# Leaving out the products of zeros on TensorE in a two-block network kernel on one core

## The chip, the core and the metric

The kernel runs on one NeuronCore of a Trainium2 chip. A core has a matrix engine (TensorE, called PE in the profile; its weight loads are the rows PEld), a vector engine (DVE), an activation engine (ACT), GpSimd (POOL) and SyncE (SP), which here only starts DMA transfers. Each engine has its own queue of instructions and runs it in order; the engines meet only at semaphores. The metric is the device time of one launch in microseconds. The shorter the better.

## The reference

The program is a chain of two small networks on 256 tokens of width 1024, all in fp32. Cut to what matters:

```
x = first_block(x)     # layer 0: gated mixer, PEER experts; layer 1: differential attention, PEER experts
x = second_block(x)    # retention + RWKV-7 mixer, cross attention to a memory, squared-ReLU MLP

h = rmsnorm(x, g) * (1 + scale) + shift          # ahead of every large product
p = h @ w_in                                     # large products: 1024 x 1536 up to 1024 x 4096
x = x + gate * (mixer(p) @ w_out)
x = x + gate * peer(h)                           # scores of 16384 experts by u, weighted sum of v
y = rmsnorm(x, norm_final)
```

Between the large products stand small ones (attention heads of 64 to 256 channels, a chunked linear recurrence with 64-step chunks, group norms), each of them bound to vector and activation work before and after it. Nothing in the reference asks for a product with zeros.

## The kernel before, in words

Activations stay in SBUF with channels on partitions and the 256 tokens along the free axis. A large product is a stream of weight tiles of 128 x 1024 (`linear`, lines 403 to 563; `peer_scores` and `peer_output` have the same stream written out). SP loads a tile into one of four slots, ACT copies it rounded to fp32r (line 265), DVE makes the rest (line 271), and PE multiplies high by high, high by low and low by high (line 399, 24 matmuls of 128x256 a tile; line 1367 for the experts' output).

The program is a list of blocks. At the end of a block all engines meet, and none starts on the next one before the last has come. In a row of the profile `<-PEq L1515` after a start means that PE's own queue was the last to reach the end of the block that was opened on line 1515. So the order of the work is that of the source, engine by engine, and a block is as long as its slowest engine.

The helper `keep_warm(count, bank)` (lines 227 to 231) issues `count` matmuls of a 128x128 matrix of zeros by 512 columns of a constant, into a PSUM bank that nobody reads. Nobody waits for them, and they wait for nobody, but they stand in PE's queue in order. Each appears in the trace as two records of line 231. There are 98 of them, in 34 places, of these kinds:

- At the end of `split` (line 390), three beside the rounding of a product's input, five times.
- In `linear` (line 469) one after the two matmuls L331 and L333 that add up squares over the channels, six times; likewise in `peer_output` (1388) and `norm_in_place` (1739). ACT turns the sum into a root (L342, L344), and the next large product then starts with its norm: DVE scales (L537), ACT rounds (L500), DVE makes the low part (L530 or L532), and PE follows channel block by channel block (L399).
- In `norm_in_place` (1737) one ahead of the sixteen records of L362 (eight matmuls with ones, which add up the squares); in `peer_output` (1380) one ahead of the transposes L786.
- In `block_rms` (line 1526, three or five at its end, behind L1524) and in the block that follows (L1577 in `odd_mixer`, L1842 in `retention`, L2213 in `rwkv`).
- In `rope` (1475) two at its end, behind the products L1473.
- In `rwkv` two ahead of the low-rank products L1898 to L1902 (1894), seven and twelve in the two blocks after them (1951, 1977), and in each of the two token tiles one ahead of L2114 and one ahead of L2123 (lines 2109 and 2117).
- In `setup` twelve, in `even_mixer` two and six.

In a token tile (`tile`, line 2026) the last block goes: L2103 and L2108, then L2114, which needs DVE's copy L2146 of L2103's result; then L2123 to L2129 in two halves, which need DVE's two copies L2149 of L2114's result; then L2135 to L2139, and DVE's two additions.

Of the kernel before, what the change touches and what calls it, by code (L numbers as in the profile page):

```python
# [20 lines left out]
BANK = 512  # L21
# [4 lines left out]
EPS = 1e-6  # L26
LAM_INIT = 0.8 - 0.6 * math.exp(-0.3)
LOWEST = -3.0e38
ROOT_IDLE = 1
ROOT_TABLE = "natural_log_exp_and_others"  # L30
ROUND = 1.5 * 2.0 ** 23

# [128 lines left out]
class Core:  # L161
# [62 lines left out]
        a, b = COLS[name]  # L224
        return self.cols[:, a:b] if n is None else self.cols[:, a + n:a + n + 1]

    def keep_warm(self, count, bank=7):


        for _ in range(count):  # L230
            self.nc.tensor.matmul(self.bank[bank][:], self.c("zeros"), self.const[:, 0:BANK], start=True, stop=True)  # L231


    def add_segment(self, name):
        tiles = self.dram[name]
        first = self.segments[-1].first + self.segments[-1].count if self.segments else 0
# [132 lines left out]
    def split(self, src, high, low):  # L369

        nc, rounded = self.nc, self.sig("norm_rounded")
        pairs = src.shape[1] // 2
        with nc.Block() as block:
            @block.scalar
            def _(act):
                self.first_parts(act, "high")
                for n in range(pairs):
                    nc.scalar.activation(high[:, 2 * n:2 * n + 2, :], src[:, 2 * n:2 * n + 2, :], ACT.Identity).then_inc(rounded.sem, 1)

            @block.vector  # L380
            def _(dve):
                self.first_parts(dve, "lows")
                for n in range(pairs):
                    dve.wait_ge(rounded.sem, rounded.at(n + 1))
                    nc.vector.tensor_tensor(low[:, 2 * n:2 * n + 2, :], src[:, 2 * n:2 * n + 2, :],
                                            high[:, 2 * n:2 * n + 2, :].bitcast(F32), ALU.subtract)

            @block.tensor
            def _(pe):
                self.keep_warm(3)  # L390
        rounded.close(pairs)

    def product(self, out, slot, rhs, k, start, stop):
# [9 lines left out]
    def linear(self, engine, take, groups=1, rhs=None, loads=(), aside=None, per_tile=1, norm=None, squares=None, root=None):  # L403
# [11 lines left out]
        with nc.Block() as block:  # L415
# [8 lines left out]
            @block.tensor  # L424
            def _(pe):
                def begin(turn, b, g):
                    slot = (b * groups + g) % RING
                    if g == 0:

                        pe.wait_ge(free.sem, turn * RING + free.at(b + 1 - RING))  # L430

                    pe.wait_ge(sig(f"low{slot}_ready").sem,
                               turn * groups + ((b * groups + g) // RING + seg.first // RING + 1))
                    return slot

                def part(b, g, slot, c):
                    x = (rhs_high[:, g * KB + c, :], rhs_low[:, g * KB + c, :])
                    mm = self.product(self.bank[b][:, 0:T], slot, x, c, g + c == 0, g == groups - 1 and c == KB - 1)
                    if c == KB - 1:
                        mm.then_inc(used.sem, 1)  # L440

                def tiles(turn, only=range(RING)):
                    for b in only:
                        for g in range(groups):
                            slot = begin(turn, b, g)
                            for c in range(KB):
                                part(b, g, slot, c)

                if norm is None:
                    with pe.Fori(0, blocks // RING) as turn:  # L450
                        tiles(turn)
                else:

                    for c in range(KB):
                        for b in range(3 if c < 5 else 2):
                            if c == 0:
                                begin(0, b, 0)
                            if b == 0:
                                pe.wait_ge(lowered.sem, lowered.at(c + 1))
                            part(b, 0, b, c)  # L460
                    for c in range(5, KB):
                        part(2, 0, 2, c)
                    tiles(0, (3,))
                    if blocks > RING:
                        with pe.Fori(1, blocks // RING) as turn:
                            tiles(turn)
                if squares is not None:
                    self.sum_squares(pe)
                    self.keep_warm(ROOT_IDLE)

            def take_out(eng):
                def finish(i, t):
# [206 lines left out]
def setup(core):  # L679
# [5 lines left out]
    with nc.Block() as block:  # L685
# [35 lines left out]
        @block.tensor  # L721
        def _(pe):
            pe.wait_ge(tables.sem, 16)
            core.sum_parts(pe, view(core.scratch, 0, KB, T))
            core.keep_warm(12)

        @block.vector
        def _(dve):
# [95 lines left out]
def even_mixer(core):  # L824
# [17 lines left out]
    with nc.Block() as block:  # L842
# [7 lines left out]
        @block.tensor  # L850
        def _(pe):
            pe.wait_ge(gelus.sem, gelus.at(1))
            for g in range(4):
                mm = nc.tensor.matmul(mean, core.c("ones"), v[:, g, :], start=(g == 0), stop=(g == 3))
            mm.then_inc(means.sem, 1)
            core.keep_warm(2)
            pe.wait_ge(cent.sem, cent.at(1))
            for g in range(4):
                mm = nc.tensor.matmul(var, core.c("ones"), squares[:, g, :], start=(g == 0), stop=(g == 3))
            mm.then_inc(vars_.sem, 1)  # L860
            core.keep_warm(6)

        @block.scalar
        def _(act):
# [463 lines left out]
def peer_output(core, layer):  # L1328
# [14 lines left out]
    with nc.Block() as block:  # L1343
# [12 lines left out]
        def _(pe):  # L1356
# [20 lines left out]
                    tile(turn, slot)  # L1377
            for slot in range(RING):
                tile(P // RING - 1, slot, last=(slot == RING - 1))
            core.keep_warm(1, bank=3)  # L1380
            for h in range(2):
                pe.wait_ge(early.sem, early.at(h + 1))
                pe.wait_ge(late.sem, late.at(h + 1))
# [1 line left out]
                    transposes(core, pe, [tokens[:, t, d * P:(d + 1) * P] for d in (2 * q, 2 * q + 1) for t in range(TT)],  # L1385
                               [core.bank[q]], turned)
            core.sum_parts(pe, squares)
            core.keep_warm(ROOT_IDLE)

        @block.scalar  # L1390
        def _(act):
# [67 lines left out]
def rope(core, src, dst, pairs, cos, sin, clearing=False):  # L1459
# [7 lines left out]
    with nc.Block() as block:  # L1467
        @block.tensor
        def _(pe):
            for n in range(pairs):  # L1470
                if n >= 4:
                    pe.wait_ge(taken.sem, taken.at(n - 3))
                nc.tensor.matmul(core.bank[n % 4][:], core.c("rot"), src[:, 2 * n:2 * n + 2, :], start=True, stop=True) \  # L1473
                    .then_inc(swapped.sem, 1)
            core.keep_warm(2)

        if clearing:
            @block.scalar
# [28 lines left out]
def block_rms(core, src, blocks, ones, count, eps, squares, root, centre=None):  # L1507
# [5 lines left out]
    banks = blocks // 2  # L1513
    src_f, squares_f, root_f = flat(src), flat(squares), flat(root)
    with nc.Block() as block:  # L1515
        @block.tensor
        def _(pe):
# [4 lines left out]
            for n in range(banks):  # L1522
                pe.wait_ge(squared.sem, squared.at(n + 1))
                nc.tensor.matmul(core.bank[4 + n][:], core.c(ones), squares_f[:, n * BANK:(n + 1) * BANK], start=True, stop=True) \  # L1524
                    .then_inc(summed.sem, 1)
            core.keep_warm(banks + 1, bank=3)

        @block.scalar
        def _(act):
# [29 lines left out]
def odd_mixer(core):  # L1559
# [12 lines left out]

    step, act_step = sig("dve_step"), sig("lam_exped")
    with nc.Block() as block:
        @block.tensor
        def _(pe):
            core.keep_warm(3)  # L1577

        @block.vector
        def _(dve):  # L1580
            link = Chain(step, dve)
# [134 lines left out]
def norm_in_place(core, gain):  # L1716
# [4 lines left out]
    with nc.Block() as block:  # L1721
# [12 lines left out]

        @block.tensor
        def _(pe):
            core.keep_warm(1)
            core.sum_parts(pe, squares)
            core.keep_warm(ROOT_IDLE)
    kept.close(KB)  # L1740
    core.close_parts_root()

# [16 lines left out]
def retention(core):  # L1759
# [77 lines left out]
    block_rms(core, y, 4, "half_ones", 64, core.c("eps_ret"), squares, root, centre=centred)  # L1837
    gated, step = sig("gate_activated"), sig("dve_step")
    with nc.Block() as block:
        @block.tensor  # L1840
        def _(pe):
            core.keep_warm(3)  # L1842

        @block.scalar
        def _(act):
            nc.scalar.activation(squares, proj[:, 12:16], ACT.Silu).then_inc(gated.sem, 1)
# [13 lines left out]
def rwkv(core):  # L1860
# [19 lines left out]
    with nc.Block() as block:  # L1880
# [10 lines left out]

        @block.tensor
        def _(pe):
            core.keep_warm(2)
            pe.wait_ge(hidden.sem, hidden.at(1))
            for b in range(4):
                c = slice(b * P, (b + 1) * P)
# [19 lines left out]
    with nc.Block() as block:  # L1917
# [28 lines left out]
        def _(pe):  # L1946
# [1 line left out]
            for i in range(2):  # L1948
                mm = nc.tensor.matmul(core.bank[i][:], core.c("half_ones"), flat(squares)[:, i * BANK:(i + 1) * BANK], start=True, stop=True)
            mm.then_inc(summed.sem, 1)  # L1950
            core.keep_warm(7)

        @block.scalar
        def _(act):
# [17 lines left out]
    chunks = lambda x: x.rearrange("p n (c t) -> p (n c) t", t=CHUNK)  # L1972
    exped = sig("decays_exped")
    with nc.Block() as block:
        @block.tensor
        def _(pe):
            core.keep_warm(12)

        @block.vector
        def _(dve):  # L1980
            link = Chain(step, dve)
# [44 lines left out]
    def tile(t):  # L2026
# [72 lines left out]
        with nc.Block() as block:  # L2099
            @block.tensor  # L2100
            def _(pe):
# [3 lines left out]
                for g in range(2):  # L2105
                    for h in range(4 * g, 4 * g + 4):
                        at = (h % 4) * P
                        mm = nc.tensor.matmul(core.bank[1 + g][:, at + 64:at + P], inv_T[:, h, :], a_tok[:, t, hc(h)], start=True, stop=True)  # L2108
                core.keep_warm(1)
                pe.wait_ge(out_ready.sem, out_ready.at(1))  # L2110
                for g in range(2):
                    for h in range(4 * g, 4 * g + 4):
# [1 line left out]
                        mm = nc.tensor.matmul(core.bank[1 + g][:, at:at + 64], inv_T[:, h, :], LV[:, h, :], start=True, stop=True)  # L2114
                    mm.then_inc(full.sem, 1)

                core.keep_warm(1)
                pe.wait_ge(out_ready.sem, out_ready.at(3))
                for c in range(2):
                    rows = slice(64 * c, 64 * c + 64)  # L2120
# [85 lines left out]
    with nc.Block() as block:  # L2206
        @block.tensor
        def _(pe):
            for i in range(2):
                mm = nc.tensor.matmul(core.bank[i][:], core.c("half_ones"), flat(bonus_terms)[:, i * BANK:(i + 1) * BANK],  # L2210
                                      start=True, stop=True)
            mm.then_inc(full.sem, 1)
            core.keep_warm(5)  # L2213

        @block.vector
        def _(dve):
# [277 lines left out]
```

## Time and profile before

| | |
|---|---|
| median of 3 runs | 2814.22 us (2813.64 to 2818.51) |
| the profiled execution's own time | 2819.79 us |
| its span in the trace | 2817.8 us |
| PE busy | 2567.3 us, 91% |
| DVE busy | 1859.6 us, 66% |
| ACT busy | 1307.7 us, 46% |
| mean granted TensorE clock | 0.961 of full speed |
| L231, the products of zeros | 196 records, 94.7 us busy |

A granted clock of 1.00 is 2.4 GHz and one of 0.50 is 1.2 GHz; the trace has only these two, and a number in between is a stretch that holds some of both. All times of the trace are us from the span's start. A row of the timeline gives start, length, engine, line, what is written and read, how many instructions are merged, and in brackets how long the engine was idle before and who ended that. The profiled execution is 5.6 us longer than the median of the runs, and 1.3 us longer than the longest of the three.

### The profile page before, as it was taken

To read this page: it belongs to the slowest core of one execution; us is meant where nothing else is said; L and a number is where in the kernel's file an instruction comes from. 1 tells how busy PE (TensorE), PEld (TensorE's weight loads), DVE (VectorE), ACT (ScalarE), POOL (GpSimd) and SP (SyncE) were. 2 spreads that over 40 slices of the span, in tenths; PEclk is the share of its full clock that TensorE was granted. 3 is DMA by queue.
4 is the path that set the end of the run, shared out by engine and by line. 5 is a ranking of instruction groups with operands and counts; after the bars stand their busy time and mean duration, and the time that the engine had idled before them with its cause. 6 is when DMAs were issued, how large, how long until landed. Compare 5 with 4: busy or idle time off the path is not lost. (4 is left out here: it accounts for less than half of the span.)

```text
span 2817.8 us, 45777 instructions
## 1 busy us (share of the span) xinstructions
PE 2567.3 (91%) x17160; PEld 2309.7 (82%) x17160; DVE 1859.6 (66%) x3769; ACT 1307.7 (46%) x1964; POOL 498.5 (18%) x320
## 2 busy tenths in 40 slices
PE   5698999999999999689999999999999779897989
PEld 4588999997888888389999997888879468686978
DVE  6676999858777764555888757666664464544654
ACT  3345654555454453444665555555554210354343
POOL 0001666721000001000666721000000200000000
PEclk9899999999999999799999999999999898999999
DMA  8655777753777746144767643666645100242544
GB/s 344 255 172 156 211 217 221 219 171 84 265 259 265 265 163 225 43 143 141 185 181 184 182 134 91 218 217 217 218 145 185 69 1 1 75 161 78 173 135 155
DMA packets 200506, 480.68 MB, mean 171 GB/s; under 512 B 54448, under 2 KB 87728, under 8 KB 199760
## 3 DMA queue, kind: packets, MB, share of 16 engines
q1 hardware_dynamic: 150960, 432.01, 45.5%
q10 hardware_dynamic: 12576, 47.29, 4.4%
q0 software_dynamic: 36864, 0.15, 3.3%
q8 instruction: 44, 0.72, 0.1%
q14 instruction: 62, 0.51, 0.1%
HBM read 461.41 MB, written 17.96 MB: 170 GB/s over the span
## 5 line engine op out<-in xcount | busy, mean ns | idle before, releaser
L271 DVE TENSOR_TENSOR weight_low<-weight_raw,weight_high 128x1024 fp32r<-128x1024 f32 x732 | 893.0, 1222 | 429.6 <-ACT weight_high L265 424.5
L399 PE MATMUL bank<-h_high,weight_high 128*128 128x256 f32 x3552 | 1022.7, 288 | 84.5 <-DVE weight_low L271 24.8
L265 ACT ACTIVATE weight_high<-weight_raw 128x1024 fp32r<-128x1024 f32 x732 | 773.8, 1059 | 670.0 <-DMA weight_raw<-peer_v_dram 343.7
L399 PE MATMUL bank<-h_low,weight_high 128*128 128x256 f32 x3552 | 1017.3, 286 | 0.0
L399 PE MATMUL bank<-h_high,weight_low 128*128 128x256 f32 x3552 | 1016.7, 286 | 0.0
L399 PEld LDWEIGHTS bank<-h_high,weight_high 128*128 128x128 f32 x3552 | 693.8, 195 | 102.1 <-issue 84.0
L399 PEld LDWEIGHTS bank<-h_low,weight_high 128*128 128x128 f32 x3552 | 694.0, 195 | 0.0
L399 PEld LDWEIGHTS bank<-h_high,weight_low 128*128 128x128 f32 x3552 | 693.5, 195 | 0.0
L1091 POOL DMA_INDIRECT gate_table<-pick_expo,pick_spot x256 | 457.9, 1789 | 772.4 <-DVE pick_expo L1193 466.9
L1367 PE MATMUL bank<-weight_high,act_high 128*128 128x512 f32 x1024 | 318.5, 393 | 6.7 <-DVE act_low L1420 6.1
L1367 PE MATMUL bank<-weight_low,act_high 128*128 128x512 f32 x1024 | 316.9, 391 | 0.0
L1367 PE MATMUL bank<-weight_high,act_low 128*128 128x512 f32 x1024 | 316.6, 391 | 0.0
L1420 DVE TENSOR_TENSOR act_low<-arena,act_high 128x256 fp32r<-128x256 f32 x256 | 108.8, 425 | 224.8 <-ACT act_high L1398 224.7
L1367 PEld LDWEIGHTS bank<-weight_high,act_high 128*128 128x128 f32 x1024 | 191.8, 189 | 49.9 <-issue 10.2
L1367 PEld LDWEIGHTS bank<-weight_low,act_high 128*128 128x128 f32 x1024 | 193.4, 189 | 40.4
L1367 PEld LDWEIGHTS bank<-weight_high,act_low 128*128 128x128 f32 x1024 | 192.9, 188 | 40.2
L1157 ACT ACTIVATE arena<-bank 128x256 f32<-128x256 f32 x256 | 97.9, 383 | 242.9 <-PE bank L399 242.7
L566 ACT ACTIVATE arena<-bank 128x256 f32<-128x256 f32 x124 | 47.2, 381 | 154.5 <-PE bank L399 154.4
L1398 ACT ACTIVATE act_high<-arena 128x256 fp32r<-128x256 f32 x256 | 102.3, 400 | 12.3 <-PEq L1231 11.5
L231 PE MATMUL bank<-const 128*128 128x512 f32 x196 | 94.7, 619 | 14.0 <-PEq L1917 3.5
L1487 POOL TENSOR_TENSOR arena<-arena,trig 128x512 f32<-128x512 f32 x12 | 18.4, 1561 | 484.9 <-ACTq L1467 484.9
L336 ACT ACT_TABLE_LOAD x14 | 18.0, 1283 | 145.2 <-PEq L2171 123.3
(327 smaller groups left out, 2532.9 us busy)
## 6 DMA issues: line engine op xcount, KB each, us to landing
weight_raw<-peer_u_dram SPq DMA_DIRECT2D x256, 512.0 KB
weight_raw<-peer_v_dram SPq DMA_DIRECT2D x256, 512.0 KB
later_modulations<-ada_later_dram ACTq DMA_DIRECT2D x54, 512.0 KB, 4.4
gate_table<-later_modulations ACTq DMA_DIRECT2D x8, 2048.0 KB, 16.7
weight_raw<-peer_w_q_dram SPq DMA_DIRECT2D x32, 512.0 KB
gate_tiles<-gate_table SPq DMA_DIRECT2D x256, 64.0 KB, 3.3
weight_raw<-w_in_dram SPq DMA_DIRECT2D x32, 512.0 KB
weight_raw<-mlp_w_up_dram SPq DMA_DIRECT2D x32, 512.0 KB
```

The source lines that it names most:

```text
L231: self.nc.tensor.matmul(self.bank[bank][:], self.c("zeros"), self.const[:, 0:BANK], start=True, stop=True)
L265: self.nc.scalar.activation(self.high[:, slot, :], self.raw[:, slot, :], ACT.Identity) \
L271: eng.tensor_tensor(self.low[:, slot, :], self.raw[:, slot, :], self.high[:, slot, :].bitcast(F32), ALU.subtract) \
L336: self.nc.scalar.preload_act_table_set(ROOT_TABLE)
L399: mm = self.nc.tensor.matmul(out, w, x, start=(start and i == 0), stop=(stop and i == 2), skip_group_check=skip)
L566: return lambda n, bank: self.nc.scalar.activation(dst[:, n + offset, :], bank, func)
L1091: pool.indirect_dma_start(core.table[layer], bass.IndirectOffsetOnAxis(ap=b.spot[:, h, i:i + 1], axis=0), b.expo[:, 0, h, i:i + 1], None, ...
L1157: nc.scalar.activation(acts[:, n, :], core.bank[n % RING][:, 0:T], ACT.Gelu).then_inc(free.sem, 1)
L1367: mm = nc.tensor.matmul(out[2 * t + h][:], x[:, slot, of], w[:, slot, halves[h]], start=(first and n == 0), stop=(last and n == 2), skip_g ...
L1398: nc.scalar.activation(core.act_high[:, n % RING, :], acts[:, n, :], ACT.Identity).then_inc(rounded.sem, 1)
L1420: nc.vector.tensor_tensor(core.act_low[:, slot, :], acts[:, n, :], core.act_high[:, slot, :].bitcast(F32), ALU.subtract).then_inc(split.se ...
L1487: nc.gpsimd.tensor_tensor(dst[:, 2 * n:2 * n + 2, :], src[:, 2 * n:2 * n + 2, :], cosb, ALU.mult) \
```

## The change

The helper, its count `ROOT_IDLE` and all its calls go. No other instruction is touched and none changes its place: PE's queue keeps its order without the rows of line 231, and the other engines' queues are the same. Where a block's PE part held nothing else, the part goes as well. The diff, cut to one call of each kind:

```
-ROOT_IDLE = 1
...
-    def keep_warm(self, count, bank=7):
-        for _ in range(count):
-            self.nc.tensor.matmul(self.bank[bank][:], self.c("zeros"), self.const[:, 0:BANK], start=True, stop=True)
...
-            @block.tensor
-            def _(pe):
-                self.keep_warm(3)
         rounded.close(pairs)
...
                 if squares is not None:
                     self.sum_squares(pe)
-                    self.keep_warm(ROOT_IDLE)
...
             core.sum_parts(pe, view(core.scratch, 0, KB, T))
-            core.keep_warm(12)
...
                 nc.tensor.matmul(core.bank[4 + n][:], core.c(ones), squares_f[:, n * BANK:(n + 1) * BANK], start=True, stop=True) \
                     .then_inc(summed.sem, 1)
-            core.keep_warm(banks + 1, bank=3)
...
         @block.tensor
         def _(pe):
-            core.keep_warm(1)
             core.sum_parts(pe, squares)
-            core.keep_warm(ROOT_IDLE)
...
-            core.keep_warm(2)
             pe.wait_ge(hidden.sem, hidden.at(1))
...
-                core.keep_warm(1)
                 pe.wait_ge(out_ready.sem, out_ready.at(1))
...
-                core.keep_warm(1)
                 pe.wait_ge(out_ready.sem, out_ready.at(3))
```

## Rows read from the trace of the kernel before

**Rows 1.** The page: the group of line 231 (count, busy us, mean ns).
```profile
L231 PE MATMUL bank<-const 128*128 128x512 f32 x196 | 94.7, 619 | 14.0 <-PEq L1917 3.5
```

**Rows 2.** Stretches of PE: length, busy, records, granted clock, DMA share, GB/s.
```profile
1124.80:1131.50 6.70, 3.65 (x16) 0.50 1.02 407
...
1135.00:1138.00 3.00, 2.59 (x24) 1.00 0.00 0
...
2086.00:2095.00 9.00, 5.68 (x20) 1.00 0.00 0
...
2236.00:2243.80 7.80, 7.61 (x32) 1.00 0.00 0
...
2289.90:2323.10 33.20, 30.71 (x256) 1.00 0.00 1
```

**Rows 3.** Timeline of PE: zeros behind `rope`, sums of squares at 2081.
```profile
1120.61 1.88 PE L231 MATMUL bank<-const 128*128 128x512 f32 x4
...
2081.26 3.62 PE L362 MATMUL bank<-arena,const 128*128 128x256 f32 x16
```

**Rows 4.** Timeline of the last block of token tile 0, then of tile 1.
```profile
2325.97 3.35 PE L2108 MATMUL bank<-arena 128*128 128x64 f32 x16
...
2330.93 3.52 PE L2114 MATMUL bank<-scratch,arena 128*128 128x64 f32 x16
...
2334.48 0.69 DVE L2149 COPY arena<-bank 128x512 f32<-128x512 f32 x1 [1.01 <-PE bank L2114]
...
2336.18 1.12 PE L2123 MATMUL bank<-arena 64*64 64x64 f32 x16
...
2344.96 0.38 PE L2139 MATMUL bank<-arena 128*64 128x128 f32 x2
...
2391.15 1.08 PE L231 MATMUL bank<-const 128*128 128x512 f32 x2
2392.06 1.89 PE L2114 MATMUL bank<-scratch,arena 128*128 128x64 f32 x16
...
2394.80 0.68 PE L2123 MATMUL bank<-arena 64*64 64x64 f32 x16
...
2400.39 0.38 PE L2139 MATMUL bank<-arena 128*64 128x128 f32 x2
```

**Rows 5.** Timeline at three block ends: start, us, engine, line, count, idle.
```profile
1132.41 2.31 PE L231 MATMUL bank<-const 128*128 128x512 f32 x5
...
1133.55 0.15 DVE L1588 TENSOR_SCALAR arena<-arena 128x1 f32<-128x1 f32 x1
...
1188.31 1.91 ACT L1537 ACTIVATE arena<-arena 128x2048 f32<-128x2048 f32 x1
1188.67 3.17 PE L231 MATMUL bank<-const 128*128 128x512 f32 x7
...
2227.30 1.88 PE L231 MATMUL bank<-const 128*128 128x512 f32 x4
2227.36 1.06 ACT L1537 ACTIVATE arena<-arena 128x1024 f32<-128x1024 f32 x1
```

**Rows 6.** Timeline: one kind of matmul at low and at high clock.
```profile
87.57 3.43 PE L854 MATMUL bank<-arena,const 128*128 128x256 f32 x8 [3.17 <-ACT arena L865]
...
1148.75 1.22 PE L1638 MATMUL bank<-arena 128*128 128x256 f32 x2 [0.58 <-ACT arena L1702]
...
1153.46 0.70 PE L1638 MATMUL bank<-arena 128*128 128x256 f32 x2 [0.58 <-ACT arena L1702]
...
2088.84 3.72 PE L362 MATMUL bank<-arena,const 128*128 128x256 f32 x16 [0.63 <-ACT arena L355]
```

**Rows 7.** Stretches: the first 72 matmuls of L399 after a norm.
```profile
1036.80:1048.40 11.60, 11.50 (x72) 0.74 0.08 22
...
2095.30:2104.30 9.00, 8.86 (x72) 1.00 0.05 8
2459.60:2469.90 10.30, 10.25 (x72) 0.85 0.04 8
```

## What the change does to the time: the prediction

> **What bounds the kernel now.** I read the page first. PE is busy for most of the span and no other engine comes near (the table of the page), so whatever slows PE's matmuls by a share slows the kernel by nearly that share, wherever PE is the engine waited for. The products of zeros hold PE for 94.7 us in 196 records [rows 1]. Most of that is idle time filled up: PE has to wait anyway for DVE and ACT between the large products. So the change asks two questions. Where does a zero product stand ahead of something that is ready, so that time is given back? And where does its absence leave PE quiet so long that the next matmuls run at half clock?
>
> For the first I went through the timeline at each of the 34 places and looked at what ended last before the block's end. For the second I went through the stretches by granted clock. Away from the long streams the clock drops to 0.50 again and again, zero products or not. At 1124.80 it is low, although four records of zeros ended at 1122.49, only 2.3 us before, and it stays so while PE does sixteen records of transposes [rows 2, 3]. It is low too at 2325.97, right behind and beside small matmuls [rows 4]. The zeros thus keep the clock at some places and not at others, and only the places where the row shows 1.00 now have something to lose.
>
> **What is given back.** (a) Four block ends at which PE's queue comes last. At 1134.72 the zeros end (1132.41 + 2.31), while DVE's last small operation ended at 1133.70: about 0.8 us after the cost of the meeting, which both pay. At 1191.84 the zeros end, ACT's exponential at 1190.22, and the next block opens when PE's queue comes: 1.6 us. At 2229.18 they end, ACT at 2228.42: 0.8 us; the same block comes a second time at 2411 with the same lengths: 0.8 us [rows 5]. Sum 4.0 us. What is late next is ACT or DVE by the ends just named; at the other block ends DVE or ACT ends last already, and there the removal gives nothing. Their cover is the longest at the five input roundings and in the two blocks of `rwkv` with seven and twelve products.
>
> (b) In the token tiles the zeros stand inside the chain. In tile 0, L2108 ends at 2329.32 and its successor L2114 was ready long before, but starts at 2330.93: PE's last record of L2108 would have been followed at about 2329.1, so 1.8 us. DVE's second copy ends at 2335.17 and L2123 starts at 2336.18: 1.0 us. In tile 1 at full clock the first product costs 0.9 us (2391.15 to 2392.06) and the second 0.1 [rows 4]. Sum 3.8 us. (c) The product ahead of the transposes in `peer_output` ends within 0.3 us of DVE's copy that they wait for; twice, I take 0.4 us. Given back in all: 8.2 us.
>
> **What the clock takes.** I price only places that are at 1.00 now and would have nothing to fill a quiet stretch.
>
> (d) `norm_in_place`. The stretch from 2086 to 2095 is at 1.00 throughout with 20 records in it, four of them zeros [rows 2]. Without them PE is quiet from 2084.9, where the first sum of squares ends, to 2088.8 [rows 3, 6], 3.9 us, while at 1124.80 the clock was found low after 2.3. Sixteen records of L362 take 3.72 us now; at low clock eight of the same size took 3.43 us [rows 6], so sixteen take 6.9: 3.1 us more, all of it on the path, for the root waits for the last of them. The stream behind it opens with 72 matmuls in 8.86 us; the same opening took 10.25 us with the clock low for a first part and 11.50 with it low for longer [rows 7]. I take 1.4 us. Together 4.5.
>
> (e) Two more openings, at 2491 and 2604, run at 1.00 with the same 72 matmuls (the row of 2095 stands for all three), with one zero product ahead of each: 1.4 us each, 2.8. Those that are low in part already (as 1036 and 2459) [rows 7] get 0.5 in all.
>
> (f) Attention of layer 1. The first scores take 2.59 us for 24 records at 1.00 [rows 2], with the six records of zeros directly ahead. At low clock the first head's share of it is some 0.9 us later. Two heads after 1152 run at 1.00. Their L1638 takes 0.70 against 1.22 us in the head before [rows 6], 0.5 us, of which ACT and DVE cover some; I take 0.35 a head. Together 1.6.
>
> (g) The low-rank products of `rwkv`, 32 records in 7.61 us at 1.00 [rows 2], behind zeros in three blocks in a row. Without those PE is quiet from before 2227 [rows 5] to 2236, some 9 us. They are four rounds, each made of six slots one after the other. L1638 is of the same size and goes from 0.70 to 1.22 us a pair when the clock is low [rows 6], 0.26 us a record. 24 slots by 0.26 are 6.2 us if the clock stays low, and a third of that if it rises after the first round or two. PE is the slower side there. I take 5.0.
>
> (h) The transposes behind `rope` in the second mixer, eight records: sixteen take 3.65 us at low clock [rows 2], half of it at high, so eight cost 0.9 more. I take 0.8.
>
> (i) The token tiles. Tile 0 is at low clock already from L2108 on, tile 1 at high. L2114 takes 3.52 against 1.89 us, and from L2123's start to L2139's end it is 9.16 against 5.97 us [rows 4]: 4.8 us. Tile 1 loses its zeros at just the two waits at which small matmuls leave PE least to do, so I count the 4.8 in full; if L2108 too is slow (3.35 us in tile 0, of which 1.4 is the low clock) it is 6.2, and zero if it holds its clock. The norm behind it (L1520, L1524) may then start low: between 0 and 2.6 us (four records by 0.4 and two more waits), I take 1.0.
>
> (k) Hidden: in `even_mixer` the sum of squares L859 would be slow, but DVE does its window sums for the pooling before it asks for the root; the sum L1949 in `rwkv` ends before DVE's scan does. Price 0; without that cover 1.5 us (eight records, half of 3.43 saved now [rows 6]) and 0.9. The twelve products of `setup` are followed by a long wait and a low clock already: 0. The first stream after `even_mixer` starts 0.4 us ahead of a low stretch: 0.2.
>
> Sum of the losses: 4.5 + 2.8 + 0.5 + 1.6 + 5.0 + 0.8 + 4.8 + 1.0 + 0.2 = 21.2 us. Less 8.2: 13.0 us slower than the profiled execution, 2819.8 + 13.0 = 2832.8. That execution lies 5.6 us above the median, and a part of this may be tile 0, whose low clock need not come in every run; in the changed kernel such luck helps less, since fewer products keep the clock. So I take off only a third of the difference and say 2831 us, 0.6% over the median before.
>
> **A rule against the trace.** After the transposes of 1124.80 to 1131.50, the only work in that stretch, the clock is 1.00 at 1135.00 [rows 2], and it was up before the zeros began. The Trainium skill, "TensorE: Matmul & The Clock Gate", Part 4 on the PE-mode transpose, says that transposes don't count as activity for the clock gate. By that rule the first products of the tiles, which stand right behind 32 records of transposes, would start low once the zeros ahead are gone, some 4 us more by the rows of tile 0. The trace disagrees with the rule, so I leave this out of the sum.
>
> **The rivals.** First, the other side: no slower than before, because the clock falls by itself. At 1124.80 the clock was low although zeros had run just before, so they may be too few to hold it, and chance decides at 2086, 2236 and in tile 1. Then the 8.2 us given back stand against the places that are certain (f, h, k: 2.6) and half of d and e, 3.9. 2819.8 - 8.2 + 6.5 = 2818, and with the median's luck 2813 to 2815: no change. It decides once the losses stay under 14 us. For it: about half of the zeros' places are low afterwards today. Against: the stretch from 2086 to 2095 and that from 2236 are at 1.00 without a break, and with the zeros taken out they hold more quiet time than places that fell.
>
> Second, the clock stays down for long once it is down. In the tiles the six levels (L2069 to L2080) are 33 us a tile of small matmuls nearly without a pause, at 1.00 now [rows 2]. If they all ran low, at L1638's ratio of 1.7, they would cost some 23 us more each. I take one third of one tile and all of (g) and (i): 2831 + 8 + 4 = 2843, in the worst case over 2855. Against: the dense levels and streams are at 1.00 within a few microseconds in every case now.
>
> Third, a clock that is lost but mostly hidden: DVE and ACT chains swallow half of g and i, 2831 - 6 = 2825. This lies within my forecast.
>
> **How the numbers follow.** Forecast (losses of 16 to 28 us, 2826 to 2840): 0.70, the third rival in it. First rival 0.17, second 0.10, something else 0.03. A measurement here tells a change from none at 0.2%, 5.6 us, so slower means over 2819.8 us: 0.70 + 0.10 and a little of the first rival, 0.83. Within: 0.13. Faster, below 2808.6, needs gains with no loss at all: 0.04. The range holds the forecast, the better part of the first rival's upper end and the second's lower: 2819 to 2844.
>
> **What would show it.** Right: a mean granted clock of about 0.93 to 0.94 in place of 0.961; L362 at about 2088 in 6 to 7 us; L1898 to L1902 in 11 to 13 us in place of 7.6; tile 1's L2114 in 3.5 us; the openings at 2491 and 2604 in over 10 us; DVE's start behind L1515 released by ACT instead of PE's queue. Wrong: a mean clock at or above 0.955, or L362 still in 3.7 us; or long streams with low stretches inside, which would be the second rival.

## The result, and the profile after

The changed kernel takes 2826.8 us in the median of six runs (2823.25 to 2828.94) against 2811.92 us of the kernel before in six runs (2805.29 to 2818.51). The ratio is 1.0052 with an interval of 1.0036 to 1.0069: slower by 14.9 us. The prediction said 2831. The profiled execution took 2828.94 us, 9.1 more than that of before, which was one of the long ones of its kernel.

From the page of the profile after, the span and PE's rows of parts 1 and 2:

```profile
span 2826.9 us, 45385 instructions
...
PE 2505.1 (89%) x16964; PEld 2293.4 (81%) x16964; DVE 1857.6 (66%) x3769; ACT 1308.1 (46%) x1964; POOL 512.3 (18%) x320
...
PE   4598999999999998599999999999989568697978
...
PEclk8799999999999999599999999999999688898989
```

PE has 196 records and 94.7 us of zeros less [rows 1], but is only 62.2 us less busy: some 32 us came back as longer matmuls. The mean granted clock is 0.937 in place of 0.961. DVE and ACT are as busy as before to 2 us. POOL has 13.8 us more, but its busy time differs by as much between two profiles of the kernel before (498.5, and 514.5 in e5 below). What changed is on PE.

Stretches of PE in the kernel after, with the columns of [rows 2]:

```profile
1120.90:1127.40 6.50, 2.78 (x13) 0.50 1.02 406
2083.50:2092.00 8.50, 6.54 (x16) 0.61 0.01 2
2093.70:2104.00 10.30, 10.20 (x72) 0.84 0.03 4
2232.90:2250.00 17.10, 13.88 (x32) 0.50 0.00 0
2285.00:2335.90 50.90, 44.12 (x420) 1.00 0.01 1
...
2496.40:2506.90 10.50, 10.35 (x72) 0.84 0.04 7
2609.50:2621.90 12.40, 11.18 (x72) 0.74 0.03 7
```

The second row answers to the stretch from 2086 in [rows 2] and to the sixteen records that took 3.72 us [rows 6]; the third, sixth and seventh to the opening of 72 matmuls that took 8.86 us [rows 7]; the fourth to the low-rank products at 2236 in [rows 2]. All of these were at 1.00.

The timeline of PE in the kernel after, at the same places (start, length, line, count, idle before and who ended it). L354 was L362, L1868 to L1872 were L1898 to L1902:

```profile
2084.47 6.54 PE L354 MATMUL bank<-arena,const 128*128 128x256 f32 x16 [3.95 <-ACT arena L347]
...
2093.80 0.55 PE L388 MATMUL bank<-h_high,weight_high 128*128 128x256 f32 x1 [2.79 <-DVE h_low L518]
...
2235.34 0.79 PE L1868 MATMUL bank<-arena 64*128 64x256 f32 x1 [8.78 <-ACT arena L1856]
...
2236.49 1.22 PE L1871 MATMUL bank<-arena 128*128 128x256 f32 x2
```

The first three rows show the pattern: an idle time of 2.8 to 8.8 us that no zeros break, and behind it matmuls that start at half clock. The fourth is from the middle of the low-rank products and is still slow.

To find where the 9.1 us between the two profiled executions arise I compared the length of every block, from its opening to the next one's, in the two traces. Differences in us (after less before); the last column is the time at low clock in the block, before and after:

| block, by its line before | difference | low clock |
|---|---|---|
| 1515, the third sum and its end, at 1180 | -2.45 | 5.5, 3.9 |
| 1515, in `retention` and `rwkv` | -0.77 each | 0, 0 |
| 1574, `odd_mixer` | -0.77 | 0, 0.1 |
| 1721, `norm_in_place` | +2.82 | 0, 6.8 |
| openings behind it and at 2489 and 2602 | +1.36, +1.45, +2.08 | 0, 3.4 to 6.8 |
| ten other openings together | -0.1 | |
| 1607, attention | +1.43 | 32.1, 43.8 |
| 801 behind `rope`, at 2198 | +0.82 | |
| 1880, low-rank products | +6.27 | 0, 17.8 |
| tile 0, last block (2099) | -5.74 | 17.1, 6.8 |
| tile 1, first (2035), last (2099), states (2171) | +1.45, +3.78, +0.93 | 0, 3.4 to 10.2 |

What is left comes to -2.6 us; the largest are -1.1 at 801 (at 2276), -1.1 at 1128 (at 228), +0.7 and -0.6 in the two blocks behind that, -0.7 in `retention` and +0.6 at 842. These are of the size by which two profiles of the same kernel differ.

The longest low stretch of the kernel after, from 2230.1 to 2284.8, reaches over the low-rank block and the three behind it. Before, there were two in that part, 3.4 and 6.8 us long. Only the low-rank block got longer by it: the next two take as long as before to 0.1 us, and the third is 1.1 us shorter.

### The profile page after: what moved, and what is told of

It is laid out like the page before. It is cut to its first block and busy times, and to the rows that moved or that the text cites. A ratio compares the mean times of both kernels' runs of the same rounds, so it can differ in the third digit from the quotient of the medians.

```text
span 2826.9 us, 45385 instructions
## 1 busy us (share of the span) xinstructions
PE 2505.1 (89%) x16964; PEld 2293.4 (81%) x16964; DVE 1857.6 (66%) x3769; ACT 1308.1 (46%) x1964; POOL 512.3 (18%) x320
## 5 line engine op out<-in xcount | busy, mean ns | idle before, releaser
L1076 POOL DMA_INDIRECT gate_table<-pick_expo,pick_spot x256 | 471.9, 1844 | 755.3 <-DVE pick_expo L1178 468.4
L388 PE MATMUL bank<-hidden_high,weight_high 128*128 128x256 f32 x256 | 73.7, 288 | 16.1 <-PEq L365 16.1
```

Of the source, the lines that this page charges most:

```text
L388: mm = self.nc.tensor.matmul(out, w, x, start=(start and i == 0), stop=(stop and i == 2), skip_group_check=skip)
L1076: pool.indirect_dma_start(core.table[layer], bass.IndirectOffsetOnAxis(ap=b.spot[:, h, i:i + 1], axis=0), b.expo[:, 0, h, i:i + 1], None, ...
```

## The experiments

The two sets of runs had their own runs of the kernel before: 2812.14 us in 29 runs beside e1 to e4, and 2813.89 us in 23 beside e5 to e8. My theory: the loss is half clock at a few places, and each such place can be bought back alone. The rivals: something diffuse, or single places that matter less than the trace suggests, because a low clock only moves on to the next place.

**e1: zeros only where the prediction priced the clock** (`split`, `setup`, `even_mixer`, line 1380, and the two later blocks of `rwkv` and line 2213 lose theirs).

```diff
@@ split
-            @block.tensor
-            def _(pe):
-                self.keep_warm(3)
@@ setup
-            core.keep_warm(12)
@@ even_mixer
-            core.keep_warm(2)
-            core.keep_warm(6)
@@ peer_output
-            core.keep_warm(1, bank=3)
@@ rwkv
-            core.keep_warm(7)
-            core.keep_warm(12)
@@ rwkv, behind the tiles
-            core.keep_warm(5)
```

> The kernel before, with zeros left only at the places where I priced a loss (roots of the norms, norm in place, rope, block norms, the two blocks ahead of the low-rank products, the token tiles); gone are those of setup, even mixer, the five input roundings, the seven and twelve and the last five of rwkv, and the one ahead of the transposes in the experts' output. Theory (only some places hold the clock, the rest fill waits that end in a low clock anyway): same as the kernel before within 2 us, mean granted clock 0.95 to 0.96, low-rank block 11.5 us, norm-in-place block 6.7 us. Rival (every zero product adds its share to holding the clock): 49 of 98 products gone, so about half of the loss of 15 us, 7 us slower than before.

Measured: 2815.87 us, ratio 1.0011 (0.9995 to 1.0027). These 74 of the 196 records do most of the work; the 3.7 us over are more than I expected, and the interval (-1.4 to 7.6 us) doesn't tell them from my bound of 2. The clock (0.949 to 0.954) and the two blocks (11.52 and 6.70 us) came as expected. The expectation miscounts: 122 records are 61 of the 98 products, not 49, so the rival's share of 14.9 us would be 9.3, which lies outside the interval.

**e2: the complement**, zeros only at the places that e1 empties, 122 records. Its diff is that of the change without those calls.

> The complement of the first: zeros only in setup, even mixer, the input roundings, the seven, twelve and five of rwkv, and ahead of the transposes. Theory: the full loss, as the changed kernel (0.5% over before), clock 0.935 to 0.942. Rival (each product adds its share): 7 us over before, clock about 0.95.

Measured: 2826.25 us, ratio 1.006 (1.0039 to 1.0082), as slow as with no zeros at all. Its low-rank block is 17.79 us long and its norm block 9.50, the kernel after's lengths. So the five roundings, `setup`, `even_mixer` and the later blocks of `rwkv`, 122 of 196 records, buy nothing here that can be measured. The prediction had priced them at 0 with the work that hides them. The clock missed its expectation: 0.949 to 0.951 in the six runs, where 0.935 to 0.942 was expected and the kernel after shows 0.937 to 0.940. These zeros raise the mean clock by 0.01 and the time is the same, so the mean clock alone doesn't tell what a place is worth.

**e3: the kernel after, with the zeros of `norm_in_place` and of the two roots back.**

```diff
@@ after, linear, behind the sum of squares
+                    self.keep_warm(ROOT_IDLE)
@@ after, peer_output
+            core.keep_warm(ROOT_IDLE)
@@ after, norm_in_place
+            core.keep_warm(1)
             core.sum_parts(pe, squares)
+            core.keep_warm(ROOT_IDLE)
```

> The changed kernel with zeros back only behind the sums of squares and ahead of the one in norm in place (two places in norm_in_place, linear, peer_output). Clock theory: L362 in norm in place 3.7 us and not 6.8, its block 6.7 us again, the three openings at 1.00 back to 8.9 us; 7 to 9 us faster than the changed kernel. Rival (the slow openings come from something else that shifted, such as transfers or DVE): the blocks keep their length, under 2 us gained.

Measured: 2820.52 us, ratio 1.0036 (1.0021 to 1.0051), 6.3 us under the kernel after by the medians and a little under the 7 to 9 expected. The two were not measured in one set; by their ratios, each against its own runs of before, the gain is 4.5. Timeline of PE in e3 around `norm_in_place` (L396 is the stream's matmul):

```profile
2076.87 3.62 PE L362 MATMUL bank<-arena,const 128*128 128x256 f32 x16
2080.33 1.02 PE L231 MATMUL bank<-const 128*128 128x512 f32 x2
2082.72 1.10 PE L231 MATMUL bank<-const 128*128 128x512 f32 x2 [1.37 <-PEq L1337]
2084.44 3.72 PE L362 MATMUL bank<-arena,const 128*128 128x256 f32 x16 [0.63 <-ACT arena L355]
2088.00 1.02 PE L231 MATMUL bank<-const 128*128 128x512 f32 x2
2090.96 0.35 PE L396 MATMUL bank<-h_high,weight_high 128*128 128x256 f32 x1 [1.94 <-DVE h_low L527]
```

Three products of zeros (two records each) stand in the 3.95 and 2.79 us of quiet that the kernel after has here; no idle time is longer than 1.94, and the sixteen records are back at 3.72 us from 6.54. The norm block is 6.70 us again, its opening 1.33 shorter, the last one (2602) 2.10. These three make 6.25 us. The third opening that was to come back, the one at 2489, did not: with its product of zeros in place it takes 52.16 us (52.09 in the kernel after, 50.64 before), with a low stretch of 3.4 us in it.

**e4: the kernel after, with the zeros of `retention`'s end and of the start of `rwkv` back.**

```diff
@@ after, retention
+        @block.tensor
+        def _(pe):
+            core.keep_warm(3)
@@ after, rwkv
+            core.keep_warm(2)
             pe.wait_ge(hidden.sem, hidden.at(1))
```

> The changed kernel with zeros back only in the gate block of retention (three) and ahead of the low-rank products of rwkv (two). Clock theory: that block goes from 17.8 us back to about 11.5 us, nothing else moves by more than 1 us, so 5 to 7 us faster than the changed kernel. Rival (the clock is lost already in the block norm before, whose zeros stay out): block still over 15 us, under 3 us gained.

Measured: 2819.8 us, ratio 1.0035 (1.0020 to 1.0050), 7.0 us under the kernel after by the medians, 4.8 by the ratios. The timeline of PE in e4 (L1881 to L1885 are the low-rank products):

```profile
2225.08 2.81 PE L231 MATMUL bank<-const 128*128 128x512 f32 x6 [2.11 <-PEq L1505]
2229.29 1.96 PE L231 MATMUL bank<-const 128*128 128x512 f32 x4 [1.39 <-PEq L1822]
2231.75 0.48 PE L1881 MATMUL bank<-arena 64*128 64x256 f32 x1 [0.51 <-ACT arena L1868]
...
2232.39 0.70 PE L1884 MATMUL bank<-arena 128*128 128x256 f32 x2
...
2238.67 0.69 PE L1885 MATMUL bank<-arena,scratch 32*128 32x256 f32 x2
```

Five products, none of which is the last to end in its block, are worth the whole block: 17.79 us down to 11.52. Other blocks moved by up to 1.6 us, more than the 1 expected. If e3 and e4 add up, which was not run, they bring back 13.3 of the 14.9 us by the medians, 9.3 by the ratios.

**e5: the kernel before once more, for a second profile**, for the question whether the low clock in the last block of tile 0 [rows 4] was an accident of that one profile.

> The kernel before, unchanged, for a second profile. Theory (the profiled execution of before was slow by chance in token tile 0, where its clock was low for 17 us): in this one the last block of tile 0 takes 14.9 to 18 us in place of 22.8, and the time is near the median of 2812. Rival (tile 0 is always slow in this kernel): 22.8 us again.

Measured: 2816.84 us. The block was 22.8 us long again, with L2114 at 3.51 us. The theory of an accident missed here. The same profile shows what else the first one can't be trusted for: attention (1607) took 46.51 us in it, with 40.7 at low clock, against 45.80 and 32.1, and the block norm at 1180 took 10.44 against 11.32.

**e6: the kernel before without the two zeros of each token tile.**

```diff
@@ token tiles
-                core.keep_warm(1)
                 pe.wait_ge(out_ready.sem, out_ready.at(1))
@@
-                core.keep_warm(1)
                 pe.wait_ge(out_ready.sem, out_ready.at(3))
```

> The kernel before without the two zero products in each token tile, all others kept. Theory: tile 1's last block takes 17.0 to 18.6 us in place of 14.9, tile 0's 17 as in the changed kernel; against the median of before +2 to +5 us. Rival (the zeros stand on the chain and only delay): tile 1 at 13.9 us, 2 us faster in all.

Measured: 2818.06 us, ratio 1.0019 (1.0005 to 1.0033). In its profile tile 1's last block goes from 14.85 to 17.05 us and tile 0's from 22.81 to 21.43, where 17 was expected. Stretches of PE in e6, first from the last block of tile 1, then from that of tile 0, and below them the timeline of tile 1:

```profile
2391.00:2402.00 11.00, 9.09 (x144) 0.69 0.01 1
2323.30:2340.00 16.70, 15.92 (x168) 0.51 0.01 2
```

```profile
2386.72 1.95 PE L2108 MATMUL bank<-arena 128*128 128x64 f32 x16
2388.51 1.95 PE L2113 MATMUL bank<-scratch,arena 128*128 128x64 f32 x16
2391.24 0.68 PE L2121 MATMUL bank<-arena 64*64 64x64 f32 x16 [0.78 <-DVE arena L2147]
```

So in these profiles the zeros cost 1.4 us in the tile that is low anyway and save 2.2 in the one that is high.

**e7: the kernel before, trimmed** only where zeros are the last to end in a block or stand before ready work.

```diff
@@ peer_output
-            core.keep_warm(1, bank=3)
@@ block_rms
-            core.keep_warm(banks + 1, bank=3)
+            core.keep_warm(banks // 2 + 1, bank=3)
@@ odd_mixer
-            core.keep_warm(3)
+            core.keep_warm(2)
```

> The kernel before with fewer zeros where PE came last at a block's end: three and two in place of five and three in the block norms, two in place of three beside the lambdas, none ahead of the transposes of the experts' output. Theory: block norms end when ACT does, 1.6 + 0.8 + 0.8 us, 0.7 at the lambdas, 0.4 at the transposes: 4 us faster than before, and the clock the same. Rival (the last zeros are what holds the clock there): low-rank block or attention slower by as much.

Measured: 2804.28 us, ratio 0.9967 (0.9952 to 0.9982): 9.6 us faster than before. Of the blocks that I had trimmed three are shorter by 2.12, 0.76 and 0.76 us; the fourth (at 2406) is 0.56 longer, with a low stretch in it now. That is 3.1 us together, near the 4 expected (2.2 if the first is measured against e5). The time gained is more than twice that, and the largest single difference lies elsewhere: tile 0's last block takes 14.85 us, at full clock throughout (stretch of PE in e7, then the timeline there, L2107, L2113 and L2122 being L2108, L2114 and L2123):

```profile
2318.00:2333.00 15.00, 13.37 (x203) 1.00 0.01 3
```

```profile
2318.68 1.95 PE L2107 MATMUL bank<-arena 128*128 128x64 f32 x16
2320.47 1.08 PE L231 MATMUL bank<-const 128*128 128x512 f32 x2
2321.38 1.89 PE L2113 MATMUL bank<-scratch,arena 128*128 128x64 f32 x16
2323.11 1.08 PE L231 MATMUL bank<-const 128*128 128x512 f32 x2
2324.12 0.56 PE L2122 MATMUL bank<-arena 64*64 64x64 f32 x12
```

**e8: e7, and more zeros where PE still stood quiet ahead of work that it bounds**: ahead of the norm openings, in the transposes' blocks, at the ends of the experts' blocks, and longer fillings where there were some.

```diff
@@ split
-                self.keep_warm(3)
+                self.keep_warm(min(3 + pairs, 15))
@@ linear, ahead of the opening with a norm
+                    self.keep_warm(1)
@@ setup
-            core.keep_warm(12)
+            core.keep_warm(18)
@@ token_major
+            if aside is not None:
+                core.keep_warm(7)
@@ even_mixer
+            core.keep_warm(2)
...
-            core.keep_warm(6)
+            core.keep_warm(11)
@@ peer_queries, peer_scores, peer_weigh, at the end of PE's part
+            core.keep_warm(5)
...
+            core.keep_warm(3)
...
+            core.keep_warm(2)
@@ rope
-            core.keep_warm(2)
+            core.keep_warm(min(pairs, 7))
@@ rwkv
-            core.keep_warm(7)
+            core.keep_warm(10)
...
-            core.keep_warm(12)
+            core.keep_warm(17)
@@ token tiles, at the end of each level's block
+                core.keep_warm(1)
```

> The trimmed kernel with more zeros in the waits that ended at a low clock: before the openings of the large products, behind the key scores and the experts' gates, in rope, in the token-major blocks and in the waits of rwkv, each as long as PE's slack there. Theory (the quiet is what costs the clock): low stretches fall from 222 us to under 100, mean clock over 0.975, openings at 8.9 us, 15 to 30 us faster than before. Rival (the zeros delay more than the clock gives back, or the low stretches are hidden anyway): within 5 us of before.

Measured: 2776.7 us (2772.17 to 2782.98), ratio 0.9878 (0.9859 to 0.9897): 37 us faster than before and 50 faster than the kernel after, the fastest of all and above the 15 to 30 expected. From its page:

```profile
span 2781.0 us, 46121 instructions
...
PE 2607.7 (94%) x17332; PEld 2306.2 (83%) x17332; DVE 1858.0 (67%) x3769; ACT 1307.1 (47%) x1964; POOL 511.8 (18%) x320
...
PEclk9999999999999999699999999999999999999999
```

The zeros of e8 are 368 records, 170.0 us, nearly twice those of before, and the program is shorter. The clock is low for 98 us in all, where it was for 222. One opening in e8, on the timeline of PE and as a stretch:

```profile
158.90 1.02 PE L231 MATMUL bank<-const 128*128 128x512 f32 x2
160.83 1.10 PE L231 MATMUL bank<-const 128*128 128x512 f32 x2 [0.92 <-PEq L415]
162.53 0.36 PE L399 MATMUL bank<-h_high,weight_high 128*128 128x256 f32 x1 [0.60 <-DVE h_low L533]
```

```profile
162.50:172.00 9.50, 8.87 (x72) 1.00 0.39 144
```

The same opening in the kernel before:

```profile
163.01 0.55 PE L399 MATMUL bank<-h_high,weight_high 128*128 128x256 f32 x1 [1.99 <-DVE h_low L532]
```

```profile
163.00:174.00 11.00, 10.99 (x70) 0.73 0.26 106
```

With one more product of zeros ahead of it, and longer fillings in the blocks before, the block is 2.68 us shorter. Which of e8's edits does how much was not taken apart. Eight such openings give 15 us in all between the two profiles, tile 0 another 8; the latter e7 had already.

**All ten traces together.** The same blocks, sorted by whether the zeros at the place are in the kernel:

| block, by its line before | with zeros | without |
|---|---|---|
| 1721, `norm_in_place` | 6.70 in seven profiles | 9.50 to 9.54 in three |
| its opening, at 2094 | 96.65 to 97.08 in seven | 98.04 to 98.22 in three |
| opening at 2602 | 97.08 to 97.26 in seven | 99.29 to 99.35 in three |
| 1880, low-rank products | 11.52 or 11.53 in seven | 17.79 in three |
| 2099, tile 1 | 14.85 in five | 16.99 to 18.63 in five |
| opening at 2489 | 50.5 to 50.7 in four, 52.0 to 52.2 in three | 51.8 to 52.1 in three |
| 801 behind `rope`, at 2198 | 2.06 in six | 2.88 in two, 2.06 in two |
| 2099, tile 0 | 14.85, 14.85, 18.14, 22.81, 22.82 | 17.06 to 17.10 in four, 21.43 |

In the first five rows the two groups don't overlap, so there the zeros hold the clock. In the last three they don't decide alone.

## Why the prediction was right, and where its sizes were off

The time came out 4.2 us under the forecast, inside its own range, and through the mechanism that it named: PE quiet longer, then matmuls at half clock where PE is waited for. That the sum comes so near is in part luck, as the terms show. By its terms, with the differences of the blocks:

- (a) Given back at four block ends: 4.0 predicted, 4.8 measured (0.77, 2.45, 0.77, 0.77). The 0.77 came out as worked out from the ends; at 1188 a part of the 2.45 is L1524, which ran with less low clock. It did so in e5 too, without any change: against e5 the block is 1.57 shorter, where 1.6 was predicted, and the four come to 3.9. In that block DVE now starts at 1187.40 (it was 1192.14), 0.3 us after ACT's exponential ends at 1187.11. So ACT is what is late, although the row still names PE's queue:

```profile
1185.20 1.91 ACT L1518 ACTIVATE arena<-arena 128x2048 f32<-128x2048 f32 x1
1187.40 2.35 DVE L1688 SCALAR_TENSOR_TENSOR arena<-arena 128x2048 f32<-128x2048 f32 x1 [6.37 <-PEq L1497]
```

- (b), (i) Token tiles. Tile 1's last block lost 3.8 us net, and with the 1.0 given back that is 4.8 in all, the number predicted, but this is luck: the step behind the number failed. The low clock began later than I had said. L2114 (now L2078), for which I had named 3.5 us as the sign, stayed at 1.95; the clock fell behind it, at 2394.0, and stayed down for 10.2 us:

```profile
2391.18 1.95 PE L2078 MATMUL bank<-scratch,arena 128*128 128x64 f32 x16
2393.92 1.09 PE L2086 MATMUL bank<-arena 64*64 64x64 f32 x16 [0.78 <-DVE arena L2112]
```

  In the other four kernels without the tiles' zeros the block takes 16.99 to 17.12 us, with 6.8 at low clock: a loss of 2.1 to 2.3 and not 3.8. The first block of tile 1 (+1.45) and the states (+0.93) I had left out; both come long or short with the tiles' zeros and without them (6.34 or 7.8 us, 4.22 or 4.8 to 5.2), so they aren't shown to be the change's doing. Tile 0 gained 5.7 us where I had 2.8, since its low stretch shrank from 17.1 to 6.8 us. In e6 and e7 the same block was 21.4 and 14.9 us long. This is the part of the result that no experiment settled.
- (c) Ahead of the transposes in `peer_output`, 0.4: no block shows it apart, and it stays untested alone (e7 holds it among its three edits).
- (d) `norm_in_place` 3.1 and its opening 1.4 predicted; 2.82 and 1.36 measured, and e3 gives them back. These are the best shown of all terms, with (g).
- (e) Two openings at 1.4 each: 1.45 and 2.08. In the second the clock fell for twice as long. The first is low also in e3, e6 and e7, with its zeros there, so the match isn't shown to be the zeros' doing. The other ten, 0.5, gave -0.1.
- (f) Attention 1.6: 1.43, but half of this is the profile of before. In e5, the same kernel, the block takes 46.51 us and not 45.80, and in e1, e6, e7 and e8 46.50 to 46.54. Against those the kernel after (47.23) loses 0.7, and e2, which lacks the same zeros ahead of it, takes 46.54. So the row with the two heads at 1.00, on which the price rested, was the exception, and the term is at most half as large. In the kernel after L1638 (now L1615) stays at 1.22 us, as the clock is low from 1137.9 to 1182.3; in e5 it is low from 1139.0 to 1183.4:

```profile
1155.90 1.22 PE L1615 MATMUL bank<-arena 128*128 128x256 f32 x2 [0.58 <-ACT arena L1679]
```

- (g) The low-rank products: 5.0 predicted, 6.27 measured, and 6.2 had been the working for a clock that stays down. I had hoped for a rise after a round or two. The clock was 0.50 over all 32 records. The mis-sized part was the reduction, not the row.
- (h) 0.8 predicted, 0.82 measured, again with luck: e2 and e4 lack the same zeros behind `rope` and take 2.06 us there, as before.
- The norm behind the tiles, 1.0: nothing, the block is at full clock and 0.77 shorter.
- (k) Cover that holds: e2 shows that 122 records at the roundings, in `setup` and in the two mixers are worth nothing together. 842 is 0.6 us longer. Against the kernel before, e1 leaves the same records out and is 3.7 us slower, with an interval that holds 0; a price of a few microseconds is not excluded.

Terms of the forecast on one side and the trace on the other: 13.0 against 9.1 us from profile to profile, a difference of 3.9. Tile 0 (2.9), the norm behind (1.0), the block ends (0.8) and the blocks that I had no term for (2.6) made the loss smaller than forecast; the first block and the states of tile 1 (2.4) and (g) (1.3) made it larger, and the rest are small. So the errors came to 7.3 one way and 3.7 the other. Against the medians the change is 14.9, close to the 16.8 of the forecast. I had taken off a third of what the profile of before was above its median; the rest of it was partly chance of the runs shown, as their median over six is 2811.92.

The first rival (the clock falls by itself, zeros or not) was wrong at its places: 2086 and 2236 fell to 0.50 only without zeros, and e3 and e4 raised both again. Chance of the kind it had in mind does show, but elsewhere: in tile 0, in attention, behind `rope` and at the opening at 2489. The second (the clock stays down long) is contradicted where it had its price, by the row of 50.9 us at 1.00 over the six levels of tile 0. Long low stretches do come, 54.7 us from 2230.1 and 44.4 from 1137.9, but they lie where PE is mostly not waited for. The third (half of (g) and (i) hidden) has the nearest number, 2825, but not the mechanism: (g) came in full.

On the rule weighed: in the kernel after, PE has only transposes between 1120.90 and 1131.00, at 0.50 in the first stretch shown above, and behind it:

```profile
1127.70:1131.00 3.30, 0.33 (x3) 1.00 1.03 413
```

And ahead of the first products of tile 0 PE does nothing but 32 records of transposes, after 25.77 us of quiet. The first half of them is at low clock, and it rises while they run:

```profile
2281.49 5.27 PE L773 MATMUL bank<-const,arena 128*128 128x128 f32 x32 [25.77 <-PEq L1943]
```

```profile
2281.00:2284.80 3.80, 3.31 (x16) 0.51 0.00 0
```

The products behind them lie in the stretch at 1.00 from 2285. The 4 us that the rule of the Trainium skill, "TensorE: Matmul & The Clock Gate", Part 4, would have cost there did not come.

## What to carry to other kernels

Go through the places where the clock is high and ask what keeps it so; price each by the same instruction in a low stretch of the same trace, and add up only where PE is the one waited for: a stretch of 54.7 us at half clock lengthened one block of the four under it. Take more than one profile of the kernel before, as a place can be high in one and low in the next. Products of zeros pay where a quiet time of some microseconds stands ahead of a run that PE bounds, and they should be counted out so that they end before the work that they wait with: in this kernel five of them were worth the 6.27 us of one block, 61 nothing that could be measured, and one too many at a block end cost 0.8 us. Before taking them out, try more of them: the trace's low stretches are the list of places.

## What the runs showed that I had not expected

- PE can be busy nearly without a pause and at half clock all the same: in e6, 15.92 of 16.70 us with 168 small matmuls at 0.51, while e7 runs the same block, zeros included, at 1.00 in 13.37 us of work. It isn't the zeros at the place alone that decide, since before, e5 and e7 have the same ones there and differ by 8 us. Whether e7's trimming causes this or the moment at which the block starts is open; there are two profiles of the kernel before and one of each other.
- The spread of a kernel's runs goes with the clock, though what sets the clock of a run isn't shown: the 23 runs of before beside e5 to e8 go from 2803.96 to 2824.00 us, and the longer ones show the lower granted clock (2805.98 us at 0.965, 2818.27 us at 0.961). The six runs of the kernel after lie within 5.7 us.
- Low clock moves. In e3 and e4 the blocks with zeros put back win what they should, all but the one at 2489, and others that were not touched shift by 0.5 to 1.6 us in either direction; in e1 the last block of tile 0, whose zeros it keeps, is 4.7 us shorter than before. A difference of one block in one profile is no proof at that size; the same length in several kernels that share an edit is.
